# Three residual norms worked by halves of the tokens, with the products around them made half by half

## The reference

```python
h = x
y = hybrid_mixer(rmsnorm(h, g[0]), ...)            # ends in  concat(...) @ w_out
h = h + rmsnorm(y, g[1])                            # first residual norm ...
y = memory_cross_attention(rmsnorm(h, g[2]), ...)   # q = (.. @ w_q); softmax; o @ w_o
h = h + rmsnorm(y, g[3])                            # second residual norm ...
y = conv_glu_ffn(rmsnorm(h, g[4]), ...)             # u = causal_dwconv(h @ w_up, 3 taps) + b; (silu(a) * b) @ w_down
h = h + rmsnorm(y, g[5])                            # third residual norm ...
# second block
shift, scale, gate = split(silu(c) @ w_ada + b_ada)
h2 = rms_norm(h, norm_g) * (1.0 + scale) + shift
proj = h2 @ w_in                                    # columns hq, hf, hi, hz, rq, ...
f = lb + (1 - lb) * sigmoid(hf); k = 1 - f; logf = log(f)   # b = running sum of logf in chunks of 64 tokens... ; q = silu(hq)
```

## Time and profile before

| what | value |
|---|---|
| median of three executions | 3482.2 us |
| the profiled execution | 3480.85 us |
| its span | 3479.0 us |
| mean granted TensorE clock | 0.927 |
| PE busy | 3008.3 us (86%) |
| VectorE busy | 1648.7 us (47%) |
| ScalarE busy | 698.5 us (20%) |
| GpSimd busy | 933.9 us (27%) |
| `out`, from first to last matmul | 840.33 to 934.3 us |
| `q` | 1002.01 to 1091.98 us |
| `o` | 1172.85 to 1265.3 us |
| first two up groups | 1338.70 to 1427.67 us |
| last down product ends | 2134.3 us |
| `hf` | 2213.66 to 2303.7 us |
| `hq` | 2312.03 to 2400.7 us |

### The profile page before, as it was taken

One profiled execution on the slowest core, in us unless ns is written; L12 is line 12 of the kernel. 1 busy time (PEld: TensorE's weight loads), 2 busy tenths in 40 slices (PEclk: granted clock), 3 DMA queues, 4 the chain that ended last, 5 costly groups with the idle time before them and its releaser, 6 DMA issues.

```text
span 3479.0 us, 45020 instructions
## 1 busy us (share of the span) xinstructions
PE 3008.3 (86%) x18988; PEld 2710.1 (78%) x18988; DVE 1648.7 (47%) x2077; ACT 698.5 (20%) x1134; POOL 933.9 (27%) x508
## 2 busy tenths in 40 slices
PE   6999788876769857999899994798999999989887
PEld 6889677766757856777777773577999999978887
DVE  3689366663131125444444444531245665555445
ACT  3010112212132222000000001331122222233331
POOL 7332231112111112223232231132323223212343
PEclk9997899898979987999999997799999999999999
DMA  5122221101220021111111113233233423245662
GB/s 189 56 92 72 90 65 41 43 31 37 87 101 25 25 97 68 43 36 52 44 38 47 36 48 115 97 121 109 82 107 104 122 92 98 98 158 188 219 243 89
DMA packets 138959, 304.74 MB, mean 88 GB/s; under 512 B 10136, under 2 KB 76592, under 8 KB 138672
## 3 DMA queue, kind: packets, MB, share of 16 engines
q10 hardware_dynamic: 102512, 170.32, 14.3%
q1 hardware_dynamic: 36288, 132.14, 11.7%
HBM read 224.81 MB, written 77.61 MB: 87 GB/s over the span
## 4 chain that ended last, share of the span: by engine, by line
PE 71%; DVE 13%; issue 6%; ACT 3%; DMA 2%; POOL 2%; ACTq 2%; DVEq 0%
PE pp L201 28%; PE pp L216 23%; PE pp L1610 6%; PE pp L1954 3%; POOL w_lo L2515 1%; PE pp L1126 1%; PE pp L1135 1%; PE pp L1137 1%; PE pp L1514 1%; DVE ffn_cb L536 1%; PE pp L1494 1%; DVE gdn_C L1312 1%; PE pp L418 1%; PE pp L1158 1%; DMA close_m<-ma_s 1%
## 5 line engine op out<-in xcount | busy, mean ns | idle before, releaser
L2513 POOL CAST w_hi<-w_raw 128x1024 fp32r<-128x1024 f32 x252 | 292.0, 1159 | 2498.8 <-PE pp L201 1055.2
L216 PE MATMUL pp<-w_hi,act_hi 128*128 128x256 f32 (+1 forms) x2752 | 801.2, 291 | 53.6 <-ACT hg_st L1823 22.7
L216 PE MATMUL pp<-w_lo,act_hi 128*128 128x256 f32 (+1 forms) x2752 | 789.3, 287 | 0.0
L216 PE MATMUL pp<-w_hi,act_lo 128*128 128x256 f32 (+1 forms) x2752 | 789.3, 287 | 0.0
L2515 POOL TENSOR_TENSOR w_lo<-w_raw,w_hi 128x1024 fp32r<-128x1024 f32 x252 | 648.6, 2574 | 20.2
L216 PEld LDWEIGHTS pp<-w_hi,act_hi 128*128 128x128 f32 x2752 | 543.6, 198 | 61.3 <-ACT hg_st L1823 22.9
L216 PEld LDWEIGHTS pp<-w_lo,act_hi 128*128 128x128 f32 x2752 | 543.2, 197 | 0.0
L216 PEld LDWEIGHTS pp<-w_hi,act_lo 128*128 128x128 f32 x2752 | 542.4, 197 | 0.0
L201 PE MATMUL pp<-act_hi,w_hi 128*128 128x512 f32 x1408 | 437.9, 392 | 31.5 <-ACTq L90 18.7
L201 PE MATMUL pp<-act_lo,w_hi 128*128 128x512 f32 x1408 | 436.2, 391 | 0.0
L201 PE MATMUL pp<-act_hi,w_lo 128*128 128x512 f32 x1408 | 436.0, 391 | 0.0
(11 more groups left out here) (373 smaller groups left out, 3946.0 us busy)
## 6 DMA issues: line engine op xcount, KB each, us to landing
w_raw<-in_weights SPq DMA_DIRECT2D x252, 512.0 KB, 3.6
z_s<-hg_st ACTq DMA_DIRECT2D x24, 1024.0 KB, 4.6
hg_qkb<-hT_s ACTq DMA_DIRECT2D x24, 512.0 KB, 6.2
qkvT_s<-mixin_o ACTq DMA_DIRECT2D x12, 512.0 KB, 2.8
gdn_qkv<-qkvT_s ACTq DMA_DIRECT2D x8, 768.0 KB, 5.6
front_x<-in_x ACTq DMA_DIRECT2D x8, 512.0 KB, 7.1
norm_mix_x<-in_x ACTq DMA_DIRECT2D x8, 512.0 KB, 3.6
x_s<-mix_y ACTq DMA_DIRECT2D x8, 512.0 KB, 2.6
```

Source lines behind the costliest of these rows:

```text
L216: last = pe.matmul(dst, a[:, k, t * P:(t + 1) * P], w[slot][:, k * SC:k * SC + n], start=(k == 0 and a is high and w is w_hi), stop=(k == ...
L2513: pool.tensor_copy(hi, raw).then_inc(w_split, 1)
```

## The change

- The two pairs `RowProduct` and `Norm` become a stage `ProductNorm`, and `Ffn` takes the third norm. None of these three ends in a barrier; those of the delta rule, `Queries`, attention and `HgInputs` stay.
- `out`, `q`, `o`, `hf` and `hq` are made for tokens 0 to 511 and then for 512 to 1023, with `product_half` (24 matmuls of 512) in place of `product_T`. Their strips stand twice in the stream: 146 strips in place of 126. The first up group is made by halves too, from two strips that stay in their slots.
- The norm of the first four tiles runs beside the product's second half; that of the last four runs in the first part of the next product. PE makes a tile's eight transposes between products of it. ScalarE and VectorE have the norm's parts of several tiles interleaved in an order written out by hand.
- `Ffn` is written out without loops. The last two groups' down products are accumulated in PSUM, tile by tile (`nine`, `ten`), and added once. The first group's down product is copied to `ffn_y` instead of added to zero. `mod` is loaded near the start of the stage; its scale part is made into the gain (1 + scale) x gain in the delta rule.
- `HgInputs` has 16 jobs of half size for `hf` and 16 for `hq`, four buffers of each kind. ScalarE takes four logarithms in a row and four sigmoids in a row. `hq`'s products wait for a free bank, not for the whole of `hf`. `LATE` is now issued here, behind the high parts of the last tile.

```diff
+        class ResidualNorm:
...
+            def first(self, act, t):
+                F.done(act.activation(self.sq[:, :], self.y[:, t, :], ACT.Square, accum_out=self.small[:, t, 0:1]), "ssy")
+                after(act, F, "ssy", t)
+                F.done(act.activation(self.small[:, t, 1:2], self.small[:, t, 0:1], ACT.Sqrt, bias=EPS, scale=1.0 / D), "rty")
...
+            def second(self, act, t):
+                after(act, self.G, "x1", t)
+                act.dma_start(x_s[t * P:(t + 1) * P, :], self.y[:, t, :]).then_inc(norm_kept[t], 16)
+                if t + self.slots < NT:
+                    self.load(act, t + self.slots)
+                S.done(act.activation(self.sq[:, :], self.y[:, t, :], ACT.Square, accum_out=self.small[:, t, 3:4]), "ssx")
...
+            def turn(self, pe, t):
+                after(pe, self.N, self.unit(), t)
+                prior(pe, self.L, "lo1", t - 2)
+                for k in range(NK):
+                    last = pe.transpose(bank(self.pairs(t)[k // 4])[:, (k % 4) * P:(k % 4 + 1) * P], self.xn[t % 2][:, k * P:(k + 1) * P], ident[:, :])
+                self.T.done(last, "turned")
...
+        class ProductNorm(Stage):
+            barrier = False
...
+            def pe(self, pe):
+                k = 0
+                for half in range(2):
+                    for s in range(N_OUT):
+                        j = self.first + half * N_OUT + s
+                        weights_ready(pe, j)
+                        for i in range(self.HT):
+                            prior(pe, self.kept, "kept", k - 4)
+                            self.made.done(product_rows(pe, j % 2, half * self.HT + i, bank(2 * (k % 4))[:, 0:SC], frees=(i == 0)), "made")
+                            k += 1
+                        if half and s < N_OUT - 1:
+                            for t in ((0,), (1, 2), (3,))[s]:
+                                self.norm.turn(pe, t)
...
+                for i in range(HT):
+                    keep(2 * n - HT + i)
+                    after(act, self.kept, "kept", 2 * n - HT + i)
+                    R.first(act, HT + i)
+                    if i:
+                        R.second(act, HT + i - 1)
+                R.second(act, NT - 1)
...
+        class Queries(Stage):
...
+                for j in range(2 * NK):
+                    h, m = j // NK, j % NK
+                    strip = FIRST_STRIP["q"] + j // 2
+                    if m == 0:
+                        R.ready(pe, h)
+                    weights_ready(pe, strip)
+                    prior(pe, self.acts, "kept", j - 4)
+                    self.pes.done(product_half(pe, strip % 2, m % 2, bank(2 * (j % 4)), h, frees=(m % 2 == 0)), "q")
+                    if j < NT // 2:
+                        R.turn(pe, NT // 2 + j)
...
         class Ffn(Stage):
...
+                weights_ready(pe, j9)
+                after(pe, V, "lo", g9 * 2 + 1)
+                nine(0, frees=True)
+                weights_ready(pe, j10)
+                after(pe, V, "lo", g10 * 2)
+                ten(0, (0,))
+                nine(1)
+                ten(1, (0,))
+                after(pe, V, "lo", g10 * 2 + 1)
+                ten(0, (1,))
+                ten(1, (1,))
+                for t in range(2, 6):
+                    nine(t)
+                    ten(t)
+                    if t >= 4:
+                        N_.turn(pe, t - 4)
+                nine(6)
+                nine(7)
+                ten(6, frees=True)
+                N_.turn(pe, 2)
+                ten(7)
+                N_.turn(pe, 3)
...
         class HgInputs(Stage):
...
             def act(self, act):
...
+                R.high(act, 6)
+                R.high(act, 7)
+                for t, name in LATE:
+                    act.dma_start(full(t), d[name]).then_inc(late_loaded, 16)
+                R.settled(act)
                 act.dma_start(self.lb[:, 0:2, :], d["lb_cols"]).then_inc(self.loaded, 16)
                 act.wait_ge(self.prep, 3)
                 act.activation(self.lb[:, 2:4, :], self.lb[:, 2:4, :], ACT.Exp).then_inc(self.prep, 1)
...
+                for j in range(4):
+                    sig(j)
+                for g in range(0, self.JOBS, 4):
+                    for j in range(g, g + 4):
+                        after(act, V, "clamp", j)
+                        self.lns.done(act.activation(self.l[j % 4][:, :], self.f[j % 4][:, :], ACT.Ln), "ln")
+                    for j in range(g, g + 4):
+                        after(act, V, "b", j)
+                        store(j, 1, self.k, self.kbst)
+                        store(j, 2, self.b, self.kbst)
+                    for j in range(g + 4, min(g + 8, self.JOBS)):
+                        sig(j)
...
             def dve(self, dve):
...
+                R.scale(dve, 4)
+                R.scale(dve, 5)
+                R.normalise(dve, 4)
+                R.scale(dve, 6)
...
-    out += [*strips(w["w_out"][0], 0, N_OUT), *strips(w["xa_w_q"][0], 0, N_OUT), *strips(w["xa_w_o"][0], 0, N_OUT)]
+    for m in ("w_out", "xa_w_q", "xa_w_o"):
+        for half in range(2):
+            out += [*strips(w[m][0], 0, N_OUT)]
...
-    for c0, n in ((hf, D), (hq, D), (hi, D), (rq, 512), (rk, 512), (rv, D), (hz, D), (ga, D), (rz, D), (gb, D)):
+    for c0, n in ((hf, D), (hf, D), (hq, D), (hq, D), (hi, D), (rq, 512), (rk, 512), (rv, D), (hz, D), (ga, D), (rz, D), (gb, D)):
```

More of the change, by code:

```diff
@@ L1626, in act, with released @@
+                N_.turn(pe, 3)
+            def released(self, pe):
+                for t in range(2):
+                    after(pe, self.sums, "sum", FG * NT - NT - 1 - t)
             def act(self, act):
-                A, V = self.acts, self.dves
+                A, V, R, N_ = self.acts, self.dves, self.prev.norm, self.norm
+                for t in range(NT // 2, NT):
+                    R.high(act, t)
                 act.dma_start(self.w[:, :, :], d["ffn_cols"]).then_inc(self.loaded, 16)
-                A.start(act)
@@ L1631, in body @@
[L1631 removed]
+                R.settled(act)
+                N_.load_gains(act)
+                for g in range(FG):
                     for m in range(2):
@@ new lines, in dve, with end @@
+                conv(0)
+                for g in range(1, FG):
+                    conv(g)
+                    if g < FG - 1:
+                        for t in range(NT):
+                            total((g - 1) * NT + t, t)
+                def end(t):
+                    total((FG - 2) * NT + t, t)
+                end(0)
+                end(1)
+                dve.wait_ge(mod_loaded, 16)
+                N_.scale(dve, 0)
+                end(2)
+                N_.scale(dve, 1)
+                end(3)
```

777 lines of the change are left out of this document (395 added, 382 removed).

## The result

| what | before | after |
|---|---|---|
| median (range), four executions each | 3483.04 us (3480.15 to 3487.68) | 3328.96 us (3326.45 to 3333.17) |
| span of the profiled execution | 3479.0 us | 3325.2 us |
| mean granted clock | 0.927 | 0.949 |
| GpSimd busy | 933.9 us | 1099.5 us |

The ratio of the medians is 0.956, with an interval of 0.954 to 0.957: 154 us saved, where 170.5 were forecast (3310 us).

What follows compares the result with a forecast made beforehand. PE's products set the time, with norms bare between them: 228.2 us of holes. Savings 55+57+59.6+1−2 = 170.5 us from 3480.85 gave 3310 us; own range 3292 to 3328, wider range 3286 to 3350.

Steps and rivals of the forecast that it cites:

- The first two norms: 196.5 and 198: `out` to end of `q` 196.5 us, saving 55; `o` to the first two up groups 198, saving 57.
- Transposes at 1.04: Groups of eight transposes between PE's products take 1.04 us each, 8.3 us a norm (bounds 1.0 and 2.0 each).
- Weights at zero: Forty half strips replace twenty; the extra splits, 142 us of GpSimd, hide under PE's products and add zero.
- The third norm: Last up product to end of `hf`, norm beside products: ends at 2341 instead of 2400.73, saving 59.6 us (22 to 75).
- The waits of 6 and 12: In `hf`, PE waits 6 us at tile 4 and 12 us at the fifth product, for the first sigmoid.
- It fits by 2.5 us; the hole of 8.2 us goes.: `hf` and `hq`: rounds of 16 to 19.3 us fit four products' 21.8, so the hole ahead of `hq` goes.
- the second rival: `hf`'s round becomes the bound: at 27 us, three rounds add 16; total 3330 to 3345 us; chance 18%.
- The clock: In `hf`, a lower granted clock after the waits at tile 4 and the fifth product costs 3 us.
- GpSimd beside VectorE: Second halves' norms meet GpSimd's splits, which stretch VectorE's operations; taken as 2, 2 and 3 us for the three norms.
- The third and fourth rival: Late half strips: 3360 to 3370 us, chance 7%; twice streamed weights bound five products: about 3550, slower than before, 2%.
- The delta rule at -2 (0 to -5): Four extra operations on one row in the delta rule, with their waits, cost 2 us (0 to 5).
- Small ones: Minor terms: delta rule's extra operations −2 us, and the half as long last store +1.

Runs made afterwards that it cites:

- the run of the copies' order: The change with ScalarE copying and squaring tiles 4 to 7 of `out` and `o` before their second squares; 3319.93 us, ratio 0.953.
- the first experiment's kernel: The change without GpSimd's splits for eight strips of `hf` and the first four of `q`, computation incomplete; 3305.01 us, ratio 0.949.
- the last kernel: The change plus turned round order, gain moved, copies' order, `nine(1)` ahead of the last strip's wait, early small load and first sigmoids; 3292.74 us, ratio 0.945.
- the run that removed them alone: The change with VectorE's order in `hf` turned: scale and clamp of four jobs, then k and scan; 3308.87 us, ratio 0.949.

## Why the prediction was right, and where it was not

**That PE bounds the kernel and the norms go beside it.** Right. The forecast's largest claim, 228 us of holes replaced by a count of waits, gave 154 of 170.5 us. That the sum came so near is in part luck: misses of 30.3 us stand against gains of 13.5 that were not forecast.

**The first two norms: 196.5 and 198.** Measured 191.9 and 197.1. The wait for ScalarE's copy of tile 7 was forecast at 3 and is 3.5 in both. The move of the copies (0.5 us left) shows that its cause is the in-order queue that the prediction walked. The transposes' wait of 2 did not come in the first; the wait on the second norm's low part was 2.0 for 3. The clock's 2 us was 0.3 behind the first wait (5.75 against 5.46) and 1.7 behind the second, with 1.6 more behind the low part's wait (23.69 us for four products, 22.05 at full clock in the run of the copies' order).

**Transposes at 1.04.** Right. In `q` eight of them take what they take in attention. Of the two groups that follow a wait around `hf`, that at 2029.83 takes 1.09 and that at 2046.56 takes 1.97.

**Weights at zero.** Right; for `out` and `o` it is shown alone, with VectorE idle: the doubled stream has the products at 93.98 and 92.39 us. GpSimd's busy time rose by 165.6 us (140 to 170 forecast), and PE's one wait on `w_lo` is the one at the last group that stood in the walk.

**The third norm: 2341, 59.6 saved.** Wrong by 22.4 us, though inside its 22 to 75. The waits of 6 and 12 were right in kind and near in size (4.9 and 9.9). The walk's tail was 3.5 us short: PE waits 5.3 us for the last strip, then 3.2 and 2.6. What failed is "It fits by 2.5 us; the hole of 8.2 us goes." The term of VectorE's turn was mis-sized: 4.3 us with GpSimd beside it, where the first round's four took 5.5 on average and up to 8.3. The round takes 23 to 28 us, not 16 to 19.3. Without the splits four turns took 13.0 us, 3.3 each, as the 3.2 of the forecast has it; what was too small is the share of GpSimd. That is the second rival, which had 18%, and its mechanism is what happened, at a price of 12.4 us of holes and 5 us of clock behind them, where its text had 16 for the holes. The prediction named the sign itself, "if `hf` has a hole every four products": the holes at the ninth and thirteenth product of `hf` and the fifth of `hq` are that sign. The hole ahead of `hq` did go, and stands four products later. The runs show it from both sides: with the order turned all three holes go, and without the splits the two go whose round has none. I had priced GpSimd as a mean stretch per operation and then compared the round's sum with PE's 21.8 us. But the row that I had beside it, `hgin_k` from 0.694 to 2.781, says that one operation can wait a whole `w_lo`. Four turns with two such each would be 4 x 2 x (2.78 - 0.69) = 16.7 us over the least; the measured excess is 22.1 - 13.0 = 9.1, and the margin was 2.5.

**The clock.** Forecast 3 us for `hf`, measured 12.2. Some 7 of these stand behind the waits that the forecast had: 2.5 in the first product of `hf`, 3.0 in tile 4's transposes and the product after them, 1.9 in products five to eight, where the window has a granted clock of 0.91 and 88 matmuls where 96 fit (21.8/0.227). So 3 was too little even for the forecast's own waits. The other 5 stand behind the holes that it did not have: behind that of 5.7 us the clock is 0.87 with 85 matmuls, where the same four products have 1.00 and 98 in the first experiment's kernel, which has no hole there. Behind the hole of 1.3 us the clock is 1.00, and nothing is lost.

**GpSimd beside VectorE.** I had weighed it too lightly. The clamp's 2.50 us beside a `w_lo` of 2.45 is a wait for the rest of GpSimd's instruction, and so is every other stretch in `hf` (last section). Here the Trainium skill's "SBUF — State Buffer", Who interferes with whom, held: by it, whichever of the two engines issues first has the shared pair of ports for its whole instruction, and the other is blocked. The prediction drew only on what that section says of two inputs in SBUF; the clamp and k have one, and the section counts `tensor_scalar` among the operations that can take the pair. That the two do so is read from their stretches; no run shows the ports. For the norms the 2, 2 and 3 us of the forecast were right in size: the run without the splits has the wait ahead of `q` 2.1 us shorter, that of the last transposes ahead of `hf` 1.7 and tile 4's 4.3. It cost most where the operations stand in series with no slack.

**The third and fourth rival.** Neither holds. No half strip comes late apart from the one named.

**The delta rule at -2 (0 to -5).** The stretch is 9.9 us longer in the profiled pair, and 6.6 by the means of eleven traces. VectorE's added busy time, 257.04 - 255.4 = 1.7 us, agrees with four operations of 0.41. What the forecast put at nothing is the clock: PE's busy time there rose from 296.85 to 306.16 us for the same matmuls in this pair. Over the eleven traces it is 304.3 us on average with the operations and 298.9 without, but the run of the copies' order has them and 298.0. That the operations raise it is likely; the medians don't resolve it, and the cause stays open.

**Small ones.** The last 1073 us came out 4.9 us shorter, 1 forecast, and the first 442 us 3 us shorter, with no edit there. Over the eleven traces the third row of `mod` starts at 442.3 to 446.5, whatever the kernel, so the 3 us are within chance. No run isolates the 4.9.

## What to carry to other kernels

When work moves out of a hole and beside TensorE, ask of each place how much slack it has in series, not how much time its operations take on average: an operation of VectorE beside GpSimd's split can wait the whole of one, and a chain of ScalarE and VectorE in turn pays that at every turn. Before enlarging buffers, order such a round by kind, so that the steps that the other engine waits for come first; that gave 20 us for a dozen lines. A wait that is removed at one place in an in-order queue may stand again one product later, as it did in `q`, or one round later, as in the last kernel; check both ends of the stretch, not the wait.

## What the runs showed of the hardware

- A `tensor_scalar` of 128x512 took 0.43 us alone and 2.50 beside one `w_lo` (2.45). The running sum took 1.225 and up to 3.409.
- In `hf` and in the norms the stretch is what GpSimd's instruction still has to run when VectorE's starts, less 0.14 to 0.24 us. The clamp at 2094.30 meets a `w_lo` with 2.21 us to go and takes 2.07 more than its least; the k at 2096.83 meets a cast with 0.87 to go and takes 0.72 more; the scan at 2097.90 meets 2.33 and takes 2.18 more. In the norms it is the same. VectorE's operations of `mix` by source (minimum, median, maximum ns): the first grows by up to 2.05 us, as it meets a `w_lo`, and the second by 0.65 only, as each time it meets the last 0.8 us of a cast. So what decides is where they meet, not the form.

```profile
L365 DVE SCALAR_TENSOR_TENSOR mix_y<-mix_y,mix_small,mix_gy x8: 1284/1607/3335, 889.9 to 951.7; 128x1024 f32<-128x1024 f32 x8
...
L368 DVE TENSOR_TENSOR mix_y<-mix_x,mix_y x8: 1224/1226/1876, 892.0 to 955.0; 128x1024 f32<-128x1024 f32 x8
```

- Two kinds of operation with an input in PSUM did not stretch: the 48 for `act_lo` (L384) took 0.674 to 0.692 us and the 88 of the taps (L557) 1.280 to 1.285, though 50 of them started with over 0.5 us of a split still to run.
- GpSimd pays as well: beside the third norm a `w_lo` took 3.27 us (2.402 is the median before) and a cast 2.05 (1.039), with 1.0 and 1.15 us of a VectorE operation still to run at their starts.
- A hole of five microseconds costs more than itself, one of 1.3 did not. The 12.4 us of holes at three edges of the round came with about 5 us of lower clock, by the run that removed them alone.
- In the delta rule, with its short bursts of matmuls, the granted clock was 0.865 to 0.880 in the six traces with four more operations on another engine and 0.870 to 0.888 in the five without. The pair before and after differs by 9 us of PE's busy time, the means by 5.4. Nothing here says why.
